# End of a MoE layer: order of mixing, turning, squaring and adding on three engines

## Chip, cores and metric
One core of one Trainium2 chip runs the whole program. The metric is device time in microseconds (us), here the median of the runs shown.

## What is computed
The reference chains two small diffusion-like blocks over 512 latent and 256 context tokens with D = 1024, all in float32. The second block has two layers; each ends with a hierarchical mixture of experts (top 2 of 32), whose result is gated and added to the residual stream. Cut to what matters:

```python
def hier_moe(h, ...):                      # h: tokens x 1024
    ...                                    # two experts and two weights per token
    yb = lax.map(expert_block, (buf.reshape(n_blk, BLK, d), blk_e))
    y = yb.reshape(n_rows, d)[dest] * sw[:, None].astype(h.dtype)
    return jnp.zeros_like(h).at[stok].add(y)
# end of layer 0: 256 context and 512 latent tokens; end of layer 1: 512 latent tokens
ctx = ctx + cgt2 * f[:, :c_len]
x = x + gt2 * f[:, c_len:]
```

Layer 1 begins with an RMS norm of both streams, so it needs the sum of squares of every token over its 1024 features. The output of the program is x after layer 1.

## The kernel before
The residual stream X lies in on-chip memory with features in the partitions: 8 feature tiles of 128, by 768 tokens. The experts write their rows to a scratch tensor `yb` in HBM, one row of 1024 per token and expert. The end of a MoE layer (class `Moe`) then goes by tiles of 128 tokens, 6 in layer 0 and 4 in layer 1. For a tile `tt`:

- GpSimd (queue POOL) gathers two tiles of rows, `GA[2*tt]` and `GA[2*tt+1]`, one indirect DMA each (L3203), the 12 or 8 of them one behind the other; each has a semaphore `got[i]`.
- ScalarE weighs the first: it multiplies its rows by the first expert's weight (L3030, semaphore `weighed`).
- VectorE mixes: second rows times second weight, plus the weighed first rows (L3063, semaphore `mixed`). Both operands lie in on-chip SBUF.
- TensorE turns the mixed tile in two groups of four 128x128 transposes into one PSUM bank each (L208, semaphore `mixturned`); there are 6 banks, so from the seventh group on it also waits for `added`.
- VectorE adds: for each of the 8 feature tiles, PSUM times gate plus X into X (L3069, semaphore `added`).

In layer 0 alone there is more (object `after`, class `TokenSums`): ScalarE squares the tile of X (L278, into one of two buffers, so the square of tile t waits for the sum of tile t-2), and TensorE sums the squares over features by 8 products with a matrix of ones (L202, 16 records in the trace). When all 6 sums are there, ScalarE takes the inverse root (L233, L235).

Each engine follows its own queue in the order written. ScalarE: all 6 weighings, then all 6 squares, then the root. VectorE: mixing 0, additions 0, mixing 1, additions 1, and so on. TensorE: turn 0, turn 1, sum 0, turn 2, sum 1, turn 3, ..., with sum t-2 ahead of turn t; the last two sums follow the last turn.

Beside that, SyncE loads the first two chunks (2 MB each) of the next layer's weights `w_in_c` as soon as the first bank is turned (L415, `all_used`); behind a barrier of all engines (L118) the third part of the program begins, which SyncE opens with the third chunk (L2334). In layer 1 SyncE stores the output of each tile when its additions are done (L3337, 512 KB each), and the program ends.

Of the kernel before, what the change touches and what calls it, by code (L numbers as in the profile page):

```python
# [9 lines left out]
ALU = mybir.AluOpType  # L10
ACT = mybir.ActivationFunctionType
# [194 lines left out]
def turn4(pe, bank, srcs, ident):  # L206
    for i, src in enumerate(srcs):
        ins = pe.transpose(bank[:, i * 128:(i + 1) * 128], src, ident)  # L208
    return ins
# [2392 lines left out]

def strips(pe, A, B, left, right0, right1, kt):

# [228 lines left out]
class Moe:  # L2833
# [124 lines left out]
    def pe(self, pe, after=None):  # L2958
        K, ps, H, tiles = self.K, self.K.ps, self.norm.H, self.tiles
        self.before.over(pe)  # L2960
        pe.wait_ge(self.tables, self.TABLES)
        for k in range(KT):
            self.norm.wait_tile(pe, k)
            for j, (a, n) in enumerate(self.segments()):
                ins = pe.matmul(ps[0:36, 2 + j, 0:n], self.wr[:, k, :], H[:, k, a:a + n], start=(k == 0), stop=(k == KT - 1), skip_group_check=True)  # L2965
                if k == KT - 1:
                    ins.then_inc(self.logits, 1)
        for tt in range(tiles):
            if tt in (0, 4):
                pe.wait_ge(self.levac[tt // 4], 1)  # L2970
            ins = pe.transpose(ps[:, 4, 36 * tt:36 * tt + 36], self.LT[0:36, 128 * tt:128 * tt + 128], K.C("ident")[0:36, 0:36])
        ins.then_inc(self.lturned, 1)
        self.pe_turn(pe, 0, 2)

        pe.wait_ge(self.masked, 2)
        n = 32 * (tiles + 1)
        flat = self.M.rearrange("p t e -> p (t e)")
        pe.matmul(ps[:, 2, 0:n], K.C("tri"), flat, start=True, stop=False, skip_group_check=True)
        for u in range(1, tiles + 1):
            ins = pe.matmul(ps[:, 2, 32 * u:n], K.C("ones"), flat[:, 0:n - 32 * u], start=False, stop=(u == tiles), skip_group_check=True)  # L2980
        ins.then_inc(self.counted, 1)
        self.pe_turn(pe, 2, tiles)
        for i in range(2 * tiles):
            pe.wait_ge(self.chosen, i + 1)
            ins = pe.matmul(ps[0:ROWS, 3, 0:self.NB], self.S[:, i, :], self.A[:, i, :], start=(i == 0), stop=(i == 2 * tiles - 1))
        ins.then_inc(self.listed, 1)
        pe.wait_ge(self.index, 1)
        pe.wait_ge(self.hevac, 2 * tiles)
        self.blocks.pe(pe)
        self.when_more(pe, self.more.pe)  # L2990
        for i in range(2 * tiles):
            tt, c = divmod(i, 2)
            pe.wait_ge(self.mixed, tt + 1)
            if i >= 6:
                pe.wait_ge(self.added, 4 * (i - 5))
            if after and c == 0 and tt >= 2:
                after.pe_sum(pe, tt - 2)
            turn4(pe, ps[:, 2 + i % 6, :], [self.GA[2 * tt][:, k * 128:(k + 1) * 128] for k in range(4 * c, 4 * c + 4)], K.C("ident")
                  ).then_inc(self.mixturned, 1)
        if after:  # L3000
            for tt in range(tiles - 2, tiles):
                after.pe_sum(pe, tt)
# [9 lines left out]
    def act(self, act, after=None):  # L3012
        K, ps = self.K, self.K.ps
        self.sums.act_root(act)
        self.norm.act_shift(act)
        act.wait_ge(self.logits, 1)
        act.activation(self.LT[0:36, 0:TX], ps[0:36, 2, :], ACT.Copy).then_inc(self.levac[0], 1)
        self.act_rows(act, 0, self.tiles)
        ex, ex8 = self.sm[:, :, 12:16], self.sm[:, :, 56:64]
        act.wait_ge(self.shifted, 1)  # L3020
        act.activation(ex, ex, ACT.Exp).then_inc(self.exped, 1)
        act.wait_ge(self.shifted, 2)
        act.activation(ex8, ex8, ACT.Exp).then_inc(self.exped, 1)
        self.blocks.act_engine(act)
        self.when_more(act, self.more.act_engine)
        act.wait_ge(self.experts, 3)
        for tt in range(self.tiles):
            A = self.GA[2 * tt]
            act.wait_ge(self.got[2 * tt], 16)
            act.activation(A, A, ACT.Copy, scale=self.WTS[:, 0, tt:tt + 1]).then_inc(self.weighed, 1)  # L3030
        if after:
            for tt in range(self.tiles):
                act.wait_ge(self.added, 8 * (tt + 1))
                after.act_square(act, tt)
            after.act_root(act)

    def dve(self, dve):
        K, ps, X, MOD = self.K, self.K.ps, self.K.X, self.norm.MOD
        self.before.over(dve)
        dve.memset(self.M[:, self.tiles, :], 0.0).then_inc(self.masked, 1)  # L3040
        self.norm.dve_gains(dve)
        self.norm.dve_scale(dve)
        if self.nt == T:
            dve.wait_ge(self.logits, 2)
            dve.tensor_copy(self.LT[0:36, TX:T], ps[0:36, 3, 0:TC]).then_inc(self.levac[1], 1)
        dve.wait_ge(self.lturned, 1)
        dve.tensor_tensor(self.L, ps[:, 4, 0:36 * self.tiles].rearrange("p (t n) -> p t n", n=36),
                          K.PR(f"rb{self.layer}").unsqueeze(1).broadcast_to([128, self.tiles, 36]), ALU.add).then_inc(self.logged, 1)
        dve.wait_ge(self.logged, 1)
        self.chain = Chain(self.gate)  # L3050
        self.dve_choice(dve)
        self.dve_places(dve)
        dve.wait_ge(self.listed, 1)
        dve.tensor_copy(self.IDX[0:ROWS, 0:self.NB], ps[0:ROWS, 3, 0:self.NB]).then_inc(self.index, 1)
        self.dve_more(dve)
        self.dve_weights(dve)
        self.blocks.dve(dve)
        self.when_more(dve, self.more.dve)
        for tt in range(self.tiles):
            A, B = self.GA[2 * tt:2 * tt + 2]  # L3060
            dve.wait_ge(self.got[2 * tt + 1], 16)
            dve.wait_ge(self.weighed, tt + 1)
            dve.scalar_tensor_tensor(A, B, self.WTS[:, 1, tt:tt + 1], A, ALU.mult, ALU.add).then_inc(self.mixed, 1)  # L3063
            for c in range(2):
                i = 2 * tt + c
                dve.wait_ge(self.mixturned, i + 1)
                for k in range(4):
                    m, at = 4 * c + k, slice(tt * 128, (tt + 1) * 128)
                    dve.scalar_tensor_tensor(X[:, m, at], ps[:, 2 + i % 6, k * 128:(k + 1) * 128], MOD[:, 40 + m, tt // 4:tt // 4 + 1], X[:, m, at],  # L3069
                                             ALU.mult, ALU.add).then_inc(self.added, 1)  # L3070

    def dve_choice(self, dve):

# [411 lines left out]
```

## Time and profile before

| | |
|---|---|
| time, median of 3 runs | 4271.62 us |
| lowest, highest | 4269.14, 4275.84 us |
| span of the profiled execution | 4284.5 us |
| PE busy | 3763.7 us (88% of the span) |
| DVE (VectorE) busy | 1536.8 us (36%) |
| ACT (ScalarE) busy | 1371.9 us (32%) |
| POOL (GpSimd) busy | 199.9 us (5%) |
| mean granted TensorE clock | 0.950 of full speed |

The profile gives no time of its own for the profiled execution beside its span, which runs from the first to the last instruction. Times in it are microseconds from the span's start. PE is TensorE's products and transposes, PEld its weight loads, SPq the queue of SyncE. "x8" are eight instructions merged into one line, with the time from the first one's start to the last one's end. In brackets stands how long the engine was idle before, and what released it; a releaser is inferred. The end of layer 0's MoE runs from some 3108 to 3169 us, that of layer 1 from some 4255 us to the end.

### The profile page before, as it was taken

What the parts mean: (1) busy time and instruction counts of PE and PEld (TensorE: products, weight loads), DVE (VectorE), ACT (ScalarE), POOL (GpSimd) and SP (SyncE); (2) the same over time, 40 slices, a digit from 0 to 9 for tenths busy, and PEclk for the clock granted to TensorE, in tenths of its full rate; (3) what the DMA queues carried; (4) which work ended last, traced back from release to release, by engine and by line L of the source; (5) the groups of instructions that cost most, each with busy time, mean ns of one, the idle gap of its engine ahead of it and who ended that gap; (6) DMA issues with size and microseconds to landing.
All of it is one profiled execution on the core that took longest, in us unless ns stands there. A gap on an engine that the chain in (4) does not pass through costs nothing. (4 is left out here: it accounts for less than half of the span.)

```text
span 4284.5 us, 75829 instructions
## 1 busy us (share of the span) xinstructions
PE 3763.7 (88%) x32214; PEld 2090.7 (49%) x32214; DVE 1536.8 (36%) x3723; ACT 1371.9 (32%) x2940; POOL 199.9 (5%) x193
## 2 busy tenths in 40 slices
PE   7998678787776998998988989999969988899997
PEld 4554566666665544564566543333345454333332
DVE  3011666666664103452257231111132183211112
ACT  2002244344433113442446222222235262222222
POOL 0000000000000001110200000000012000000000
PEclk9999799999998999999999989999979999899998
DMA  5223444444443110001110249999733102799996
GB/s 209 76 83 116 103 120 113 124 125 121 121 117 122 59 66 1 20 20 67 34 44 1 102 174 391 392 391 391 315 138 93 44 1 108 273 390 391 389 393 260
DMA packets 314586, 696.03 MB, mean 162 GB/s; under 512 B 169216, under 2 KB 195968, under 8 KB 289152
## 3 DMA queue, kind: packets, MB, share of 16 engines
q1 hardware_dynamic: 293024, 612.41, 40.1%
q0 software_dynamic: 14048, 53.49, 3.6%
q10 hardware_dynamic: 7168, 25.17, 1.5%
q8 instruction: 260, 4.26, 0.4%
q14 instruction: 86, 0.70, 0.1%
HBM read 624.94 MB, written 63.71 MB: 161 GB/s over the span
## 5 line engine op out<-in xcount | busy, mean ns | idle before, releaser
L202 PE MATMUL ps<-arena 128*128 128x512 f32 (+8 forms) x4620 | 1463.3, 481 | 81.9 <-ACT arena L1137 13.8
L202 PEld LDWEIGHTS ps<-arena 128*128 128x128 f32 (+5 forms) x4620 | 787.1, 190 | 693.9 <-issue 455.3
L2608 PE MATMUL ps<-arena 128*32 128x512 f32 x9216 | 1024.2, 597 | 33.1 <-DMA arena<-in_w 28.3
L2608 PEld LDWEIGHTS ps<-arena 128*32 128x32 f32 x9216 | 306.7, 110 | 652.8 <-issue 635.9
L620 PE MATMUL ps<-arena 64*64 64x64 f32 (+1 forms) x10624 | 459.4, 239 | 154.9 <-DVE arena L1290 40.3
L620 PEld LDWEIGHTS ps<-arena 64*64 64x64 f32 x10624 | 410.2, 144 | 241.1 <-issue 105.8
L2742 DVE COPY arena<-ps 128x384 f32<-128x384 f32 x64 | 35.7, 558 | 645.7 <-PE ps L2667 645.7
L208 PE MATMUL ps<-arena 128*128 128x128 f32 x1168 | 189.9, 297 | 84.3 <-DVE arena L3063 39.6
L2718 ACT ACTIVATE arena<-ps 96x512 f32<-96x512 f32 x64 | 38.0, 594 | 626.6 <-PE ps L2608 626.6
L208 PEld LDWEIGHTS ps<-arena 128*128 128x128 f32 x1168 | 141.1, 151 | 141.0 <-issue 44.7
L600 DVE SCALAR_TENSOR_TENSOR arena<-arena 128x769 f32<-128x769 f32 x48 | 45.7, 1016 | 277.0 <-PE ps L202 276.7
L962 PE MATMUL ps<-arena 64*64 64x64 f32 x2304 | 101.5, 245 | 37.6 <-DVE arena L1290 33.9
L400 DVE SCALAR_TENSOR_TENSOR arena<-ps,arena 128x512 f32<-128x512 f32 (+1 forms) x48 | 31.8, 662 | 286.3 <-PE ps L202 286.3
L2760 DVE TENSOR_TENSOR arena<-ps,arena 64x512 f32<-64x512 f32 x64 | 43.7, 683 | 226.5 <-ACT arena L2730 226.5
L552 ACT ACTIVATE arena<-ps 128x512 f32<-128x512 f32 x64 | 31.0, 491 | 281.2 <-PE ps L202 261.4
L2730 ACT ACTIVATE arena<-ps 64x512 f32<-64x512 f32 x64 | 38.0, 594 | 244.5 <-PE ps L2608 244.5
L962 PEld LDWEIGHTS ps<-arena 64*64 64x64 f32 x2304 | 89.2, 156 | 47.6 <-DVE arena L1290 39.5
L1748 DVE TENSOR_REDUCE arena<-ps 128x1 f32<-128x768 f32 x64 | 61.3, 958 | 142.3 <-PE ps L202 142.3
L344 PE MATMUL ps<-arena 128*128 128x512 f32 (+1 forms) x208 | 85.6, 576 | 20.8 <-ACT arena L335 20.8
L2773 POOL DMA_INDIRECT arena<-htok,arena x64 | 58.1, 908 | 932.5 <-PE ps L2667 922.0
L253 ACT ACTIVATE arena<-arena 128x768 f32<-128x768 f32 (+1 forms) x32 | 24.5, 785 | 233.7 <-DVE arena L400 233.7
L216 PE MATMUL ps<-arena 128*32 128x512 f32 x576 | 78.3, 667 | 19.9 <-DMA arena<-in_w_mod 16.9
(282 smaller groups left out, 3774.3 us busy)
## 6 DMA issues: line engine op xcount, KB each, us to landing
arena<-in_w SPq DMA_DIRECT2D x192, 2048.0 KB, 28.9
arena<-in_w_mod SPq DMA_DIRECT2D x24, 2048.0 KB
arena<-in_mod_w SPq DMA_DIRECT2D x12, 2048.0 KB
yb<-arena ACTq DMA_DIRECT2D x64, 384.0 KB, 9.9
arena<-in_rwkv_w_in SPq DMA_DIRECT2D x8, 2048.0 KB
arena<-rkvg SPq DMA_DIRECT2D x38, 384.0 KB, 4.2
rkvg<-arena POOLq DMA_DIRECT2D x32, 384.0 KB, 3.0
arena<-di SPq DMA_DIRECT2D x192, 64.0 KB, 2.6
```

Of the source, the lines that this page charges most:

```text
L202: ins = pe.matmul(out, l, r, start=(i == 0), stop=(i == len(pairs) - 1))
L208: ins = pe.transpose(bank[:, i * 128:(i + 1) * 128], src, ident)
L216: ins = pe.matmul(out[32 * j:32 * j + 32, :], cs[:, 4 * half + j, :], w[:, 4 * half + j, :], start=(half == 0), stop=(half == 1))
L344: ins = pe.matmul(out, w[:, k, :], self.H[:, k, a:a + n], start=(k == 0), stop=(k == KT - 1), skip_group_check=True)
L600: dve.scalar_tensor_tensor(self.LPs[j % 2][:, k, 1:n + 1], self.XX[:, k, 1:n + 1], self.K.PR("mu")[:, 8 * j + k:8 * j + k + 1], self.H[:, ...
L620: ins = pe.matmul(out[p, :], l[p, :], r[p, :], start=(i == 0), stop=(i == len(pairs) - 1))
L962: ins = pe.matmul(out[p, :], src[p, :], ident[p, p], start=True, stop=True)
L1748: dve.tensor_reduce(mx, self.scores(n), AX.XY, ALU.max).then_inc(self.max, 1)
L2608: return pe.matmul(bank[32 * at:32 * at + 32, :], left[:, k, 32 * g:32 * g + 32], right[:, k, :], start=first, stop=last)
L2718: act.activation(self.moe.AC[i % 2][0:ROWS, :], A[0:ROWS, :], ACT.Silu).then_inc(self.silu, 1)
L2760: dve.tensor_tensor(YS[0:64, 512:1024], ps[0:64, 7, :], YS[0:64, 512:1024], ALU.add).then_inc(self.y1, 1)
L2773: pool.indirect_dma_start(out=moe.HG[i % 3][0:ROWS, :], out_offset=None, in_=self.K.scr["htok"][0:moe.nt, :], in_offset=bass.IndirectOffse ...
```

## The change
Three orders change, in both layers; no instruction is added or removed.

- VectorE: mixing 0 stands ahead of the loop, and mixing tt+1 stands ahead of additions tt.
- ScalarE: three weighings first; then square tt (after additions tt), followed by weighing tt+3. Without `after` (layer 1) the weighings stand in a row as before.
- TensorE: sum tt-2 stands behind turn tt instead of ahead of it.

```diff
-        for i in range(2 * tiles):
-            tt, c = divmod(i, 2)
+        for tt in range(tiles):
             pe.wait_ge(self.mixed, tt + 1)
-            if i >= 6:
-                pe.wait_ge(self.added, 4 * (i - 5))
-            if after and c == 0 and tt >= 2:
+            for c in range(2):
+                i = 2 * tt + c
+                if i >= 6:
+                    pe.wait_ge(self.added, 4 * (i - 5))
+                turn4(pe, ps[:, 2 + i % 6, :], [self.GA[2 * tt][:, k * 128:(k + 1) * 128] for k in range(4 * c, 4 * c + 4)], K.C("ident")
+                      ).then_inc(self.mixturned, 1)
+            if after and tt >= 2:
                 after.pe_sum(pe, tt - 2)
-            turn4(pe, ps[:, 2 + i % 6, :], [self.GA[2 * tt][:, k * 128:(k + 1) * 128] for k in range(4 * c, 4 * c + 4)], K.C("ident")
-                  ).then_inc(self.mixturned, 1)
...
         act.wait_ge(self.experts, 3)
+        for tt in range(3):
+            self.act_weigh(act, tt)
         for tt in range(self.tiles):
-            A = self.GA[2 * tt]
-            act.wait_ge(self.got[2 * tt], 16)
-            act.activation(A, A, ACT.Copy, scale=self.WTS[:, 0, tt:tt + 1]).then_inc(self.weighed, 1)
-        if after:
-            for tt in range(self.tiles):
+            if after:
                 act.wait_ge(self.added, 8 * (tt + 1))
                 after.act_square(act, tt)
+            if tt + 3 < self.tiles:
+                self.act_weigh(act, tt + 3)
+        if after:
             after.act_root(act)
...
+        self.dve_mix(dve, 0)
         for tt in range(self.tiles):
-            A, B = self.GA[2 * tt:2 * tt + 2]
-            dve.wait_ge(self.got[2 * tt + 1], 16)
-            dve.wait_ge(self.weighed, tt + 1)
-            dve.scalar_tensor_tensor(A, B, self.WTS[:, 1, tt:tt + 1], A, ALU.mult, ALU.add).then_inc(self.mixed, 1)
+            if tt + 1 < self.tiles:
+                self.dve_mix(dve, tt + 1)
...
+    def dve_mix(self, dve, tt):
+        A, B = self.GA[2 * tt:2 * tt + 2]
+        dve.wait_ge(self.got[2 * tt + 1], 16)
+        dve.wait_ge(self.weighed, tt + 1)
+        dve.scalar_tensor_tensor(A, B, self.WTS[:, 1, tt:tt + 1], A, ALU.mult, ALU.add).then_inc(self.mixed, 1)
```

`act_weigh` holds the wait and the weighing of one tile, as `dve_mix` does for the mixing.

## Rows read from the trace of the kernel before

**Rows 1.** The page: the span of the profiled execution
```profile
span 4284.5 us, 75829 instructions
```

**Rows 2.** Timeline from 3110 us, layer 0: start, length, engine, line, operation [idle before <-releaser]
```profile
3116.18 1.28 DVE L3063 SCALAR_TENSOR_TENSOR arena<-arena 128x1024 f32<-128x1024 f32 x1 [13.40 <-DMA arena<-yb,arena]
...
3117.46 1.15 ACT L3030 ACTIVATE arena<-arena 128x1024 f32<-128x1024 f32 x1 [2.74 <-DMA arena<-yb,arena]
...
3117.53 1.97 PE L208 MATMUL ps<-arena 128*128 128x128 f32 x8 [16.12 <-DVE arena L3063]
3118.59 0.95 POOL L3203 DMA_INDIRECT arena<-yb,arena  x1 [0.30 <-issue]
...
3118.68 2.16 DVE L3069 SCALAR_TENSOR_TENSOR arena<-ps,arena 128x128 f32<-128x128 f32 x8 [1.21 <-PE ps L208]
...
3120.76 1.28 DVE L3063 SCALAR_TENSOR_TENSOR arena<-arena 128x1024 f32<-128x1024 f32 x1
3121.10 1.75 POOL L3203 DMA_INDIRECT arena<-yb,arena  x1 [0.30 <-issue]
...
3123.16 0.95 POOL L3203 DMA_INDIRECT arena<-yb,arena  x1 [0.30 <-issue]
...
3125.32 1.28 DVE L3063 SCALAR_TENSOR_TENSOR arena<-arena 128x1024 f32<-128x1024 f32 x1
3126.68 1.15 ACT L3030 ACTIVATE arena<-arena 128x1024 f32<-128x1024 f32 x1 [2.96 <-DMA arena<-yb,arena]
3130.76 1.15 ACT L3030 ACTIVATE arena<-arena 128x1024 f32<-128x1024 f32 x1 [2.93 <-DMA arena<-yb,arena]
3131.82 1.98 ACT L278 ACTIVATE arena<-arena 128x1024 f32<-128x1024 f32 x2
...
3133.00 3.75 PE L202 MATMUL ps<-arena 128*128 128x128 f32 x16 [8.94 <-ACT arena L278]
...
3136.54 1.91 PE L208 MATMUL ps<-arena 128*128 128x128 f32 x8
3137.64 2.16 DVE L3069 SCALAR_TENSOR_TENSOR arena<-ps,arena 128x128 f32<-128x128 f32 x8 [11.05 <-PE ps L208]
...
3157.74 1.86 PE L208 MATMUL ps<-arena 128*128 128x128 f32 x8
...
3159.43 1.95 PE L202 MATMUL ps<-arena 128*128 128x128 f32 x16
...
3162.14 2.05 PE L202 MATMUL ps<-arena 128*128 128x128 f32 x16 [0.76 <-ACT arena L278]
...
3169.07 0.37 SPq L2334 DMA_DIRECT2D arena<-in_w_in_c  x1
```

**Rows 3.** Who waited for whom, 3100 to 3170 us: total us, times, longest
```profile
ACT arena L278 <- DVE arena L3069: 24.1, 4, 6.2
DVE arena L3069 <- PE ps L208: 23.4, 5, 11.0
```

**Rows 4.** The gathers of L3203, 3100 to 3200 us: issue to landing
```profile
DMA to landing us min/median/max: 5.0/8.1/9.6
```

**Rows 5.** DMA share in tenths, 3118 to 3170 us, 40 slices of 1.3 us
```profile
DMA  9999999999999996000000000000000000000000
```

**Rows 6.** Busy us by stretch: length, PE, PEld, DVE, ACT, POOL, granted clock, DMA share, GB/s
```profile
3132.00:3138.00 6.00, 5.00 (x23) 5.03 (x24) 0.36 (x2) 1.80 (x2) 0.00 (x0) 0.50 1.04 383
...
3138.60:3139.40 0.80, 0.00 (x0) 0.00 (x0) 0.80 (x4) 0.00 (x0) 0.00 (x0) 0.80 0.13 44
```

**Rows 7.** Timeline of PE, 3655 to 3682 us: transposes of another stage
```profile
3656.23 1.97 PE L208 MATMUL ps<-arena 128*128 128x128 f32 x16
```

**Rows 8.** Timeline from 4250 us, layer 1
```profile
4263.82 1.15 ACT L3030 ACTIVATE arena<-arena 128x1024 f32<-128x1024 f32 x1 [3.68 <-DMA arena<-yb,arena]
...
4278.70 2.16 DVE L3069 SCALAR_TENSOR_TENSOR arena<-ps,arena 128x128 f32<-128x128 f32 x8 [1.21 <-PE ps L208]
```

**Rows 9.** DMA issued from 4278 us: the last store, size, issue to landing
```profile
out<-arena SPq DMA_DIRECT2D x1, 512.0 KB, 3.2
```

More of the change, by code:

```diff
@@ L3026, in act, with act_weigh @@
         act.wait_ge(self.experts, 3)
+        for tt in range(3):
+            self.act_weigh(act, tt)
         for tt in range(self.tiles):
-            A = self.GA[2 * tt]
-            act.wait_ge(self.got[2 * tt], 16)
-            act.activation(A, A, ACT.Copy, scale=self.WTS[:, 0, tt:tt + 1]).then_inc(self.weighed, 1)
-        if after:
-            for tt in range(self.tiles):
+            if after:
                 act.wait_ge(self.added, 8 * (tt + 1))
                 after.act_square(act, tt)
+            if tt + 3 < self.tiles:
+                self.act_weigh(act, tt + 3)
+        if after:
             after.act_root(act)
+    def act_weigh(self, act, tt):
+        A = self.GA[2 * tt]
+        act.wait_ge(self.got[2 * tt], 16)
+        act.activation(A, A, ACT.Copy, scale=self.WTS[:, 0, tt:tt + 1]).then_inc(self.weighed, 1)
     def dve(self, dve):
```

## The prediction

> **What bounds the kernel now.** I read three views in this order. First the timeline of the end of layer 0's MoE, from the first gather of expert outputs to the first instruction of the third part of the program [rows 2]; then who waited for whom in the same stretch [rows 3]; then the same timeline for layer 1, where the program ends [rows 8]. What the reader is to see: no engine is full here, and the engines wait on each other in a ring. For a token tile VectorE mixes two rows (L3063, 1.28 us), TensorE turns them (L208), VectorE adds them to X (L3069, 2.16 us for eight, the next instruction 2.07 us after the first of them). The mixing of the next tile is queued behind the additions, so TensorE begins to turn only when VectorE is through with both, and VectorE then waits 1.21 us for the first bank [rows 2]. That is 4.56 us a tile (3120.76 less 3116.18, less 0.02), for 3.35 us of VectorE's work.
>
> In layer 0 a second wait is worse. TensorE's program has "sum of squares of tile 0" ahead of "turn tile 2". ScalarE squares only after it has weighed all six tiles, the last at 3130.76, since its gather landed only then. So tile 2, mixed by 3126.60 (3125.32 + 1.28), is turned from 3136.54 on, and its additions begin at 3137.64, 11.0 us late [rows 2, 3]. After that, turning tile 3 waits for the sum of tile 1, and so on: ScalarE waits for additions 24.1 us in four pieces, VectorE for turned banks 23.4 us in five [rows 3]. The sixth tile's sum ends at 3164.19 (3162.14 + 2.05), the root follows, and the third part's first load is issued at 3169.07, 4.88 us behind the sum [rows 2]. All engines meet at a barrier there, and only the prefetch of w_in_c crosses it; so what layer 0's end gains, the program gains, unless that prefetch is late.
>
> **The change in layer 0, part by part.** Numbers count tiles from 0. Nothing is added or removed: 6 weighings, 6 squares, 6 mixings, 48 additions, 48 transposes and 6 sums stay; three orders change. I rebuild the timeline with the durations of rows 2. Where the rows are silent, a landing is taken between its neighbours.
>
> Head. Mixing 0 ends at 3117.46 as before, and the prefetch, released by the first turned bank, starts as before. Mixing 1 now stands before additions 0; it needs weighing 1 and the fourth gather, both there near 3118.7: weighing 1 ends at 3118.61, and it began when the third gather had landed, 3117.46; issues stand 1.26 us apart (two of them from 3118.59 to 3121.10), so I put the fourth landing 1.25 us behind the third [rows 2]. It runs 3118.7 to 3120.0, so additions 0 start 1.3 us later than now. Queued behind that new wait are the additions, square 0 and the weighing of tile 3. Mixing 2 at 3122.0, additions 1 at 3123.3, mixing 3 at 3125.4, additions 2 at 3126.7: 11 us earlier than now, since turn 2 (from 3123.35) no longer waits for a square.
>
> ScalarE. Square 0 goes at 3122.15 (1.05 us), weighing 3 then to 3124.4, ahead of mixing 3's need. Square 1 ends at 3126.55, weighing 4 at 3127.8 (its gather lands at 3126.65), square 2 at 3129.95, weighing 5 at 3131.9, its gather being late anyway [rows 2]. The squares put ahead of weighings cost nothing, because gathers cover them; without that cover each would cost 1.05 us.
>
> Tail. Gather eleven is the last of the twelve, issued at 3123.16 and landing 9.6 us later [rows 2, 4], at 3132.8. Mixing 5 can't start before, and it now stands ahead of additions 4. So the path from the last landing is: mixing 1.28, additions 4 and 5, 2.07 + 2.16, square 1.06, sum 1.95, in all 8.5 us, ending at 3141.3 with the small gaps. Against 3164.19 that is a gain of 22.9 us.
>
> Does TensorE keep up? It needs 1.95 us for a sum at full clock (from 3159.43) and 3.54 us from a sum's start to the turn's at the lower one (3136.54 less 3133.00) [rows 2]. A turn is 1.69 us to the next sum at the lower clock (3159.43 less 3157.74) and 0.98 us at the full one (1.97 for sixteen) [rows 2, 7]. In the trace the engine works without a pause from 3133.0 to 3138.4 at a granted clock of 0.50 (1.2 GHz), and the clock rises to 2.4 GHz between 3138.6 and 3139.4 [rows 6]. Now it would work without a pause from 3123.35: turn 2, then sum 0 at the lower clock, to 3128.85; a rise near 3129, if it comes as long after the start of the unbroken work as there. Then turn 3 to 3129.8, sum 1 to 3131.7, turn 4 to 3132.6, sum 2 to 3134.5, turn 5 to 3135.5, sum 3 to 3137.4, sum 4 to 3139.35, sum 5 to 3141.3. It keeps up, with additions 5's bank 0.6 us early.
>
> One cost the diff doesn't show. In the trace the mixing of 3120.76 overlaps the issue of a gather on POOL at 3121.10, and that issue takes 1.75 us where the others take 0.95: it ends 0.8 us after the mixing does [rows 2]. The new mixings 1 and 2 fall among the last four issues too, so the last gather is issued between 0 and 1.3 us later (nothing if only one issue is caught, as now; a mixing's length if two are). I take 0.5, nearer the row that has one caught. Layer 0: 22.9 less 0.5 is 22.4 us.
>
> The Trainium skill ("SBUF — State Buffer", section "Who interferes with whom") says that a VectorE instruction with two SBUF inputs and a GpSimd instruction that reads SBUF exclude each other for a whole instruction, and that the one issued first blocks the other. The trace agrees for one direction (the 1.75 us); by that rule mixing 1, coming 0.1 us after an issue at 3118.59, would itself be held up to 0.85 us, and so mixing 2. That speaks against mixing early; the sum by it would be 0.85 us worse for the first additions, most of which the 0.7 us that additions 4 wait for mixing 5 absorbs.
>
> **Layer 1** has four tiles, no squares and no sums, and its weighings come in the same order. Weighing 1 ends at 4264.97 (4263.82 + 1.15), and the fourth gather lands about then; so mixing 1 at 4265.1, additions 0 from 4266.4, mixing 2 at 4268.4, mixing 3 at 4271.8, additions 2 at 4273.1, additions 3 at 4275.1 where they now start at 4278.70 [rows 8]. A gain of 3.5 us: three waits of 1.21 us, less 0.1. Stores: the last one takes 3.2 us to land [rows 9]; the additions of tiles 2 and 3 now end 2.1 us apart instead of 4.6. If stores ran one behind the other that costs 1.1 us, if they overlap nothing; I take nothing, since the prefetch shows two issues of one queue with the sixteen engines full under both [rows 5], and keep 2.4 to 3.6.
>
> **Sum.** 22.4 + 3.5 = 25.9 us, against the profiled execution's span of 4284.5 us [rows 1]: 4258.6. That execution is 12.9 us longer than the median of the three timed runs, 4271.62, and nothing in the stretches above tells why; I take the difference off the median: 4245.7, say 4246. A difference under 0.2% (8.5 us) can't be told from none, the three runs alone being 6.7 us apart.
>
> **The rivals.**
> (a) TensorE stays at 1.2 GHz. For it: the clock is at 0.50 in the present stage until 3138.6 [rows 6], through two turns and a sum. Then TensorE is the bound from 3123.35: six sums at 3.54 and four turns at 1.69 are 28.0 us, ending near 3151.5, a gain of 12.7 in layer 0, 16.2 in all: 4255.5. Against it: its unbroken work would last 18 us or more, where the clock has risen behind 5.4 us of it [rows 6].
> (b) The gathers land later, since they share the DMA engines with the two prefetched chunks of 2 MB, which keep these full until some 3138.8 [rows 5]. At worst the last gather ends with them: 6 us later, 19.9 in all: 4251.7.
> (c) The gain is lost at the barrier: the third part would start at 3146.2, its weights having landed by 3138.8, so 7.4 us are to spare. To eat 18 us or more they would have to come 25 us later; 4265 to 4272.
> (d) Slower than before. The place is the wait that the change adds: additions of tile t stand behind mixing t+1 and so behind gather 2t+3. Everything after the last landing takes 8.5 us; the point from which the order loses in layer 0 is a landing at 3155.7, 23 us late, and 26 us late for the program, 35 to be measurable as slower. Price: one us per us beyond; 4282 with a landing 36 us late. Against: the DMA engines are idle from 3138.8.
> (e) That the change does nothing: it would need TensorE's turn 2 to wait still for a square; but the wait on it now stands behind both turned banks.
>
> **How the numbers follow.** Chances: forecast 0.64, (a) 0.17, (b) 0.12, (c) and (e) 0.05, (d) 0.02. The likeliest gives 4246, and 4244 to 4249 by its own terms (gain 26.5 down to 23). The range goes up past (b) and (a) to 4258 and down by the runs' scatter of some 3 us to 4241. Faster 0.93, same 0.05, slower 0.02.
>
> **What would show it.** In the changed trace: additions of tile 2 near 3127 instead of 3137.6; in steady state mixing and additions back to back on VectorE with no idle from PE L208; the wait of L278 for L3069 far under 24 us; the last mixing of layer 0 right at its gather's landing; the last sum's end near 3141; the granted clock at 1.0 from about 3129; in layer 1 additions 3.35 us apart. Wrong would be: a clock of 0.50 through to the last sum (a), POOL issues stretched two or three times, or an ACT table load between a square and a weighing (now there is none between L3030 and L278).

## The result, and the profile after

The changed kernel took 4241.35 us (median of five runs, 4239.21 to 4252.89), the kernel before, timed again beside it, 4269.29 us (five runs, 4265.18 to 4275.84). The ratio is 0.9933, with a 95% interval of 0.9914 to 0.9953: 20 to 37 us less. A second series of the changed kernel, on one chip with two experiments, gave 4250.41 us (4237.42 to 4255.8) against 4273.15 (4266.28 to 4285.7), ratio 0.9945 (0.9928 to 0.9963). So it is faster, by 0.6 to 0.7% and by about what was forecast (25.9 us); how much of the 28 us between the first two medians is the change's, the total can't tell. The stages can. The first view shows busy time by stretch, of the kernel before and then of the changed one; the columns are the stretch, its length, then busy us and instructions of PE, PEld, DVE, ACT and POOL, granted clock, DMA share and GB/s. The stretches are, in this order: the recurrence of the first part (L620); all up to the first gather of layer 0's end; layer 0's end, up to the third part's first load (L2334); the third part up to layer 1's first gather; layer 1's end.

```profile
423.30:1379.50 956.20, 736.82 (x13995) 593.67 (x13996) 620.02 (x1820) 370.89 (x1143) 0.00 (x0) 0.90 0.43 121
1379.50:3108.48 1728.98, 1600.86 (x10120) 804.33 (x10116) 504.44 (x1126) 567.68 (x1046) 95.95 (x82) 0.98 0.40 153
3108.48:3169.07 60.59, 26.60 (x144) 24.24 (x144) 20.20 (x54) 17.32 (x16) 12.27 (x12) 0.64 0.47 174
3169.07:4254.73 1085.66, 1005.61 (x6704) 438.93 (x6704) 302.74 (x579) 344.02 (x611) 65.34 (x53) 0.98 0.61 229
4254.73:4284.50 29.77, 7.88 (x32) 6.28 (x32) 13.50 (x36) 4.59 (x4) 7.77 (x8) 0.50 0.64 213
```

```profile
422.90:1361.30 938.40, 730.49 (x13995) 590.82 (x13996) 620.06 (x1820) 370.52 (x1143) 0.00 (x0) 0.91 0.44 123
1361.30:3090.71 1729.41, 1602.32 (x10120) 803.58 (x10114) 504.61 (x1126) 567.14 (x1046) 95.88 (x82) 0.97 0.41 153
3090.71:3129.91 39.20, 20.61 (x144) 19.11 (x144) 19.94 (x54) 17.33 (x16) 12.06 (x12) 0.76 0.73 269
3129.91:4212.63 1082.72, 1008.19 (x6704) 438.67 (x6704) 301.75 (x579) 343.76 (x611) 65.58 (x52) 0.97 0.61 230
4212.63:4238.80 26.17, 7.88 (x32) 6.27 (x32) 13.23 (x36) 4.60 (x4) 8.03 (x8) 0.50 0.73 243
```

Layer 0's end takes 39.2 us instead of 60.6, layer 1's 26.2 instead of 29.8. That is 21.4 + 3.6 = 25.0 us, and both lie in code that the change touches. The two spans differ by 45.7 us (4284.5 less 4238.8): another 17.8 us lie in the recurrence, which has the same instructions in both, and 2.9 in the third part. The change touches no code there, and the experiments show below how far these stages scatter.

Now the end of layer 0 in the changed kernel. Mixing is L3082 here, the additions L3075, the weighing L3042; L208 (turns), L202 (sums) and L278 (squares) keep their numbers. These lines answer to [rows 2]:

```profile
3100.75 1.28 DVE L3082 SCALAR_TENSOR_TENSOR arena<-arena 128x1024 f32<-128x1024 f32 x1 [1.25 <-DMA arena<-yb,arena]
...
3104.14 1.06 ACT L278 ACTIVATE arena<-arena 128x1024 f32<-128x1024 f32 x1 [0.83 <-DVE arena L3075]
...
3105.36 1.09 PE L208 MATMUL ps<-arena 128*128 128x128 f32 x8 [1.34 <-DVE arena L3082]
...
3106.28 1.95 PE L202 MATMUL ps<-arena 128*128 128x128 f32 x16
3107.29 1.28 DVE L3082 SCALAR_TENSOR_TENSOR arena<-arena 128x1024 f32<-128x1024 f32 x1
...
3108.48 2.15 DVE L3075 SCALAR_TENSOR_TENSOR arena<-ps,arena 128x128 f32<-128x128 f32 x8
...
3115.61 1.28 DVE L3082 SCALAR_TENSOR_TENSOR arena<-arena 128x1024 f32<-128x1024 f32 x1 [1.50 <-DMA arena<-yb,arena]
...
3116.95 1.50 PE L208 MATMUL ps<-arena 128*128 128x128 f32 x8 [1.98 <-DVE arena L3082]
...
3118.25 6.78 PE L202 MATMUL ps<-arena 128*128 128x128 f32 x48
...
3121.55 1.06 ACT L278 ACTIVATE arena<-arena 128x1024 f32<-128x1024 f32 x1 [1.50 <-PE ps L202]
...
3129.91 0.37 SPq L2334 DMA_DIRECT2D arena<-in_w_in_c  x1
```

What to see: from 3104 to 3112 mixing and additions stand back to back on VectorE, and a tile takes 3.27 us (3104.02 to 3107.29). Turn 2 (3105.36) begins 0.06 us after mixing 2 ends, and sum 0 follows it. Then the last mixing starts at 3115.61, 1.50 us after VectorE was free, for the landing of the last gather, and TensorE, idle for 1.98 us, starts turn 5 behind it. Who waited for whom, against [rows 3]: the squares' wait for additions has gone from 24.1 us to 6.1, and VectorE's wait for a turned bank, 23.4 us before, isn't in the answer any more.

```profile
DVE arena L3082 <- DMA arena<-yb,arena: 16.0, 3, 13.2
...
ACT arena L278 <- DVE arena L3075: 6.1, 4, 3.3
```

The gathers of layer 0 in the changed kernel from issue to landing, against [rows 4], and the granted clock (third figure from the right) behind the last mixing:

```profile
DMA to landing us min/median/max: 4.4/6.4/11.1
```

```profile
3117.00:3119.00 2.00, 2.00 (x12) 2.00 (x13) 2.00 (x9) 0.00 (x1) 0.00 (x0) 0.62 1.05 385
3119.00:3120.00 1.00, 1.00 (x7) 1.00 (x7) 1.00 (x5) 1.00 (x1) 0.00 (x0) 0.50 1.05 389
...
3123.00:3125.10 2.10, 2.03 (x19) 1.84 (x17) 0.00 (x0) 0.94 (x2) 0.00 (x0) 1.00 0.00 0
```

And layer 1, against [rows 8]: the last sixteen additions run as one piece, 4.22 us, without the 1.21 us in between.

```profile
4229.79 1.28 DVE L3082 SCALAR_TENSOR_TENSOR arena<-arena 128x1024 f32<-128x1024 f32 x1
4230.98 4.22 DVE L3075 SCALAR_TENSOR_TENSOR arena<-ps,arena 128x128 f32<-128x128 f32 x16
```

### The profile page after: what moved, and what is told of

Its sections match the earlier page's. It is cut to its first block and busy times, and to the rows that moved or that the text cites. A ratio compares the mean times of both kernels' runs of the same rounds, so it can differ in the third digit from the quotient of the medians.

```text
span 4238.8 us, 75824 instructions
## 1 busy us (share of the span) xinstructions
PE 3754.1 (89%) x32214; PEld 2081.2 (49%) x32214; DVE 1535.5 (36%) x3723; ACT 1370.6 (32%) x2940; POOL 200.0 (5%) x193
## 5 line engine op out<-in xcount | busy, mean ns | idle before, releaser
L202 PE MATMUL ps<-arena 128*128 128x512 f32 (+8 forms) x4620 | 1459.9, 480 | 65.3 <-ACT arena L1137 14.4
L202 PEld LDWEIGHTS ps<-arena 128*128 128x128 f32 (+5 forms) x4620 | 787.4, 191 | 673.9 <-issue 445.8
L2608 PE MATMUL ps<-arena 128*32 128x512 f32 x9216 | 1027.0, 599 | 27.3 <-DMA arena<-in_w 22.4
L620 PE MATMUL ps<-arena 64*64 64x64 f32 (+1 forms) x10624 | 458.7, 240 | 145.7 <-DVE arena L1290 40.4
L620 PEld LDWEIGHTS ps<-arena 64*64 64x64 f32 x10624 | 409.1, 144 | 229.5 <-issue 101.9
L208 PE MATMUL ps<-arena 128*128 128x128 f32 x1168 | 187.4, 295 | 81.9 <-DVE arena L3082 39.9
L208 PEld LDWEIGHTS ps<-arena 128*128 128x128 f32 x1168 | 138.4, 149 | 139.3 <-DVE arena L3082 44.3
L600 DVE SCALAR_TENSOR_TENSOR arena<-arena 128x769 f32<-128x769 f32 x48 | 45.7, 1017 | 276.6 <-PE ps L202 276.4
L400 DVE SCALAR_TENSOR_TENSOR arena<-ps,arena 128x512 f32<-128x512 f32 (+1 forms) x48 | 31.8, 662 | 286.4 <-PE ps L202 286.4
L962 PEld LDWEIGHTS ps<-arena 64*64 64x64 f32 x2304 | 86.5, 153 | 48.3 <-DVE arena L1290 39.9
L1717 ACT ACTIVATE arena<-ps 128x768 f32<-128x768 f32 x64 | 51.9, 810 | 127.1 <-PE ps L208 127.0
```

What stands on the lines that cost most here:

```text
L202: ins = pe.matmul(out, l, r, start=(i == 0), stop=(i == len(pairs) - 1))
L600: dve.scalar_tensor_tensor(self.LPs[j % 2][:, k, 1:n + 1], self.XX[:, k, 1:n + 1], self.K.PR("mu")[:, 8 * j + k:8 * j + k + 1], self.H[:, ...
L620: ins = pe.matmul(out[p, :], l[p, :], r[p, :], start=(i == 0), stop=(i == len(pairs) - 1))
L962: ins = pe.matmul(out[p, :], src[p, :], ident[p, p], start=True, stop=True)
L1717: act.activation(self.PT[j % 2].rearrange("p (b i) t -> p b (i t)", b=2), ps[:, 4:6, 0:384], ACT.Copy).then_inc(self.pt, 1)
L2608: return pe.matmul(bank[32 * at:32 * at + 32, :], left[:, k, 32 * g:32 * g + 32], right[:, k, :], start=first, stop=last)
```

## The experiments

All of them are judged by two lengths read from the trace, since they are steadier than the total: from the first gather's issue to the third part's first load (layer 0's end: 60.6 us before, 39.2 after), and from layer 1's first gather to the end (29.8 and 26.2).

**Two theories of why layer 0's end got shorter.** The one that the prediction puts first is a single wait at the head of TensorE's queue: turn 2 behind a sum whose square isn't there. The other takes the stage as a ring of three engines, in which each of the three old orders closes the ring in its own place. It came from reading the old code again after the result: there TensorE waits for mixing tt first and then runs sum tt-2, so a late mixing holds back a sum as well as a turn. Six kernels keep the six other mixtures of old and new orders. Each was profiled once; three executions of the changed order took 38.7, 39.2 and 39.9 us for layer 0's end, so differences of about 1 us between kernels say nothing.

*TensorE's order alone.* The parts of the change in `act` and `dve` are undone; of the diff there stays

```diff
             pe.wait_ge(self.mixed, tt + 1)
-            if after and c == 0 and tt >= 2:
-                after.pe_sum(pe, tt - 2)
             turn4(...)                          # both banks
+            if after and tt >= 2:
+                after.pe_sum(pe, tt - 2)
```

> TensorE's order alone is changed (turn tt ahead of sum tt-2); ScalarE and VectorE keep the order of before. Measured: the end of layer 0 from the first gather's issue to the third part's first load, 60.6 us before and 39.2 us after. Ring theory (each of the three orders closes the ring in its own place, and squares wait for the sixth weighing): squares can't start before the last weighing ends, some 23.4 us in, and mixing stands behind additions; 51 us, 48 to 53. Rival, the prediction's reading (the turn of tile 2 that waits for a square is what costs): most of the gain, 44 us or less. Layer 1, from the first gather's issue to the end: 29.8 us as before, in both.

Measured: 48.0 us, and 29.1 for layer 1. The timeline of this kernel (additions L3070):

```profile
3121.97 2.16 DVE L3070 SCALAR_TENSOR_TENSOR arena<-ps,arena 128x128 f32<-128x128 f32 x8 [1.21 <-PE ps L208]
...
3126.85 3.78 PE L202 MATMUL ps<-arena 128*128 128x128 f32 x16 [4.06 <-ACT arena L278]
...
3131.52 2.16 DVE L3070 SCALAR_TENSOR_TENSOR arena<-ps,arena 128x128 f32<-128x128 f32 x8 [6.20 <-PE ps L208]
```

Tile 2's additions (3121.97) no longer wait for a square, yet 12.6 us of 21.4 are won and not all: sum 0 starts behind the sixth weighing and the first square, at 3126.85; turn 3 now stands behind it, and the additions of tile 3 wait 6.20 us (3131.52).

*ScalarE's order alone.*

```diff
+        for tt in range(3):
+            self.act_weigh(act, tt)
         for tt in range(self.tiles):
-            (weigh tt, then all squares in a loop of their own)
+            (wait for additions tt, square tt)
+            if tt + 3 < self.tiles:
+                self.act_weigh(act, tt + 3)
```

> ScalarE's order alone is changed (squares between weighings). Ring theory: the 11 us wait of tile 2's additions goes, since square 0 is there by the time tile 2 is mixed, but each tile is still mixing, sum, turn, additions one behind the other, 7.0 us each from tile 2 on; 55 us, 51 to 57. Rival (the wait for the square is what costs): the wait is gone by this alone, 49 us or less. Layer 1 29.8 us in both.

Measured: 53.6 us, and 28.6 for layer 1. The prediction's "11.0 us late" is down to 4.20 us by this alone (3121.33), and still only 7.0 us are won. In this kernel mixing is L3069:

```profile
3121.33 2.16 DVE L3075 SCALAR_TENSOR_TENSOR arena<-ps,arena 128x128 f32<-128x128 f32 x8 [4.20 <-PE ps L208]
3123.41 1.28 DVE L3069 SCALAR_TENSOR_TENSOR arena<-arena 128x1024 f32<-128x1024 f32 x1
...
3124.74 3.79 PE L202 MATMUL ps<-arena 128*128 128x128 f32 x16 [3.01 <-DVE arena L3069]
...
3129.41 2.16 DVE L3075 SCALAR_TENSOR_TENSOR arena<-ps,arena 128x128 f32<-128x128 f32 x8 [4.73 <-PE ps L208]
```

There is the link of the ring that the prediction left out: mixing 3 at 3123.41, behind it sum 1 at 3124.74, released by the mixing, behind that turn 3, and additions 3 at 3129.41, for which VectorE waited 4.73 us. And TensorE, idle for 2.6 to 3.0 us in every round, runs this sum at the lower clock: 3.79 us, where one at full clock takes 1.95.

*VectorE's order alone.*

```diff
+        self.dve_mix(dve, 0)
         for tt in range(self.tiles):
-            (mix tt)
+            if tt + 1 < self.tiles:
+                self.dve_mix(dve, tt + 1)
             (additions tt)
```

> VectorE's order alone is changed (mixing one tile ahead). Ring theory: in the old TensorE order a sum stands behind the wait for the mixing of two tiles later, so mixing ahead takes the mixing out of each of the last tiles' rings, though squares start only after the sixth weighing: 52.5 us, 48 to 54. Rival: nothing of the 11 us wait goes and only 1.2 us a tile is saved, 56 us or more. Layer 1: all of its gain, 26.2 us, in both.

Measured: 48.4 us and 25.5. The 10.8 us wait of tile 2's additions stays whole (line L3068 here), and 12.2 us are won all the same, behind it: mixing 3 is done long before, so from sum 1 on sums and turns follow each other with pauses of at most 0.62 us, and at full clock.

```profile
3116.10 3.75 PE L202 MATMUL ps<-arena 128*128 128x128 f32 x16 [10.69 <-ACT arena L278]
...
3120.75 2.16 DVE L3068 SCALAR_TENSOR_TENSOR arena<-ps,arena 128x128 f32<-128x128 f32 x8 [10.83 <-PE ps L208]
...
3121.27 1.95 PE L202 MATMUL ps<-arena 128*128 128x128 f32 x16
...
3123.06 1.04 PE L208 MATMUL ps<-arena 128*128 128x128 f32 x8
```

This is what the first theory can't give: by it 56 us or more were expected here.

*ScalarE's and VectorE's orders, TensorE's as before.*

> ScalarE's and VectorE's orders are changed, TensorE's is that of before (sum tt-2 ahead of turn tt). Ring theory: square 0 is there when tile 2 is mixed, so the sum ahead of the turn costs its own 2 to 2.5 us once, and VectorE is a tile ahead: 39 to 43 us, so TensorE's order is worth 4 us at most. Rival (the head of TensorE's queue is what costs): 47 us or more. Layer 1: 26.2 us in both.

Measured: 40.0 us and 26.1. Sum 0 stands ahead of turn 2 and at the lower clock takes 3.78 us, which costs the additions of tile 2 (L3074) 1.46 us:

```profile
3110.10 3.78 PE L202 MATMUL ps<-arena 128*128 128x128 f32 x16 [1.29 <-DVE arena L3081]
...
3114.77 2.16 DVE L3074 SCALAR_TENSOR_TENSOR arena<-ps,arena 128x128 f32<-128x128 f32 x8 [1.46 <-PE ps L208]
```

So with the two others changed, TensorE's order is worth 0.8 us by the lengths, no more than the 38.7 to 39.9 us among which the changed order scatters, though alone it is worth 12.6. The head of TensorE's queue isn't what costs, once squares and mixings are early.

*TensorE's and ScalarE's orders*, and then *TensorE's and VectorE's*:

> TensorE's and ScalarE's orders are changed, VectorE's is that of before (mixing behind additions). Ring theory: mixing, first bank, additions follow each other, 4.56 us a tile for six tiles, then square and last sum: 43 us at full clock, up to 47 at the lower one; 39.2 if VectorE's order were worth nothing. Layer 1: 29.8 us, as before.

> TensorE's and VectorE's orders are changed, ScalarE squares after all six weighings as before. Ring theory: the additions of all tiles run as in the changed kernel, but the six squares start 23.4 us in, and sums 0 to 5 follow turns 2 to 5: 45 us at full clock, up to 50 at the lower one. If ScalarE's order were worth nothing, 39.2. Layer 1: 26.2 us.

Measured: 42.5 us (layer 1: 30.3), half a us below the expected range, and 45.7 us (layer 1: 26.1). In the first, mixings follow each other every 4.1 to 4.6 us from the first to the last, and the last one starts 29.9 us after the first gather's issue, 5.3 us behind the last landing: VectorE's order is the bound. In the second, five of six mixings have started 20.4 us after the first issue, and then additions (L3069 there) wait 7.55 us for a bank that is turned behind sum 0, whose square came after the sixth weighing:

```profile
3117.93 1.99 ACT L278 ACTIVATE arena<-arena 128x1024 f32<-128x1024 f32 x2
...
3119.02 3.78 PE L202 MATMUL ps<-arena 128*128 128x128 f32 x16 [8.25 <-ACT arena L278]
...
3123.70 2.16 DVE L3069 SCALAR_TENSOR_TENSOR arena<-ps,arena 128x128 f32<-128x128 f32 x8 [7.55 <-PE ps L208]
```

| orders changed | layer 0's end, us | gain |
|---|---|---|
| none | 60.6 | |
| TensorE | 48.0 | 12.6 |
| ScalarE | 53.6 | 7.0 |
| VectorE | 48.4 | 12.2 |
| TensorE, ScalarE | 42.5 | 18.1 |
| TensorE, VectorE | 45.7 | 14.9 |
| ScalarE, VectorE | 40.0 | 20.6 |
| all three | 39.2 | 21.4 |

The three single gains sum to 31.8 us, and together they give 21.4; the pair without TensorE gives nearly all. That is the ring theory, and the first theory falls: TensorE's order is worth 12.6 and 11.1 us (48.0 and 42.5 against 60.6 and 53.6) while mixings stand behind additions, 2.7 (45.7 against 48.4) where only squares are late, and 0.8 where neither is.

**What bounds the changed kernel.** One number differs from the change: the value at which the prefetch of `w_in_c` is released.

```diff
-        self.all_used = self.mixturned, 1
+        self.all_used = self.mixturned, 8
```

> The changed kernel, with the prefetch of the two chunks of w_in_c released by the eighth turned bank instead of the first. Theory (the last gathers land late because the prefetch shares the DMA engines with them, and the last mixing waits for that): the last gather lands 6.5 us after its issue instead of 11.1, mixing 5 waits for nothing, and the end of layer 0 takes 36.5 us, 36 to 37.5, instead of 39.2; the prefetch is done before the third part's first product asks for it. Rival (gathers land late because of their own queue of twelve issues): 39.2. Second rival (the prefetch then comes too late): longer than 39.2. Total against the kernel before: 25 us + 2.7 less, ratio 0.9935.

Measured: 36.8 us and 25.7; ratio to the kernel before 0.992 (0.9903 to 0.9937). Gathers in this kernel, issue to landing, and the last mixing with the last turn:

```profile
DMA to landing us min/median/max: 5.0/6.5/6.6
```

```profile
3130.82 1.28 DVE L3082 SCALAR_TENSOR_TENSOR arena<-arena 128x1024 f32<-128x1024 f32 x1
...
3132.16 1.09 PE L208 MATMUL ps<-arena 128*128 128x128 f32 x8 [0.18 <-DVE arena L3082]
```

The longest landing is 6.6 us instead of 11.1, the last mixing waits for nothing, and TensorE's pause ahead of turn 5 is 0.18 us instead of 1.98. The prefetch is done before the third part begins: the DMA engines are idle again from some 3140, the part's first load is issued at 3144.31. This is the shortest end of layer 0 of all that were run; by the total alone its 0.992 can't be told from the changed kernel's 0.9933 and 0.9945. So the bound that is left in the changed kernel is the one that the prediction named, the last landing, and its cause is the prefetch on the same DMA engines.

> The changed kernel, with sum 3 ahead of the wait for the last mixing instead of behind turn 5. Theory (in the changed kernel TensorE idles 1.98 us for the last mixing, then its granted clock falls to 0.50 from 3117.x to 3120.x and the last three sums and the turn take 8.1 us instead of 6.9): sum 3 fills most of that idle stretch, one sum less stands behind the last mixing, the clock stays at 1.0, and layer 0's end takes 38.3 us, 38.0 to 38.6, against 39.2. If the clock falls all the same, 38.8 or more. If the tail is bound by additions, square and sum alone, 39.2. Layer 1 26.2.

```diff
         for tt in range(tiles):
+            early = after and tt == tiles - 1
+            if early:
+                after.pe_sum(pe, tt - 2)
             pe.wait_ge(self.mixed, tt + 1)
...
-            if after and tt >= 2:
+            if after and tt >= 2 and not early:
```

Measured: 39.9 us and 25.6. As a whole that is a miss, by 1.5 us: the last gather landed 26.3 us after the first issue in this execution, 24.9 in that of the changed kernel. 1.1 of these 1.4 us are a later end of the last issue (16.5 against 15.4 us), since three issues were stretched there (1.22, 1.65 and 1.71 us), and one in the changed kernel's (1.63). Behind the last mixing:

```profile
3118.98 1.29 DVE L3085 SCALAR_TENSOR_TENSOR arena<-arena 128x1024 f32<-128x1024 f32 x1 [0.76 <-DMA arena<-yb,arena]
...
3121.25 1.04 PE L208 MATMUL ps<-arena 128*128 128x128 f32 x8
...
3123.48 4.12 PE L202 MATMUL ps<-arena 128*128 128x128 f32 x32 [1.20 <-ACT arena L278]
```

```profile
3123.50:3125.60 2.10, 2.08 (x17) 1.90 (x17) 0.90 (x4) 1.15 (x2) 0.00 (x0) 1.00 0.01 4
```

Sum 3 fills the pause, the granted clock stays at 1.00, and from the start of the last mixing to the end of the last sum it is 8.6 us (3118.98 to 3127.60), against 9.4 (3115.61 to 3125.03). But that isn't shown to be the new order's doing. In the changed kernel's second execution (`e11_after_again`, below), with sum 3 behind turn 5, TensorE idled 1.08 us ahead of turn 5, the granted clock stayed at 1.00 too, and the same path took 8.6 us (3112.11 to 3120.73):

```profile
3113.45 1.09 PE L208 MATMUL ps<-arena 128*128 128x128 f32 x8 [1.08 <-DVE arena L3082]
...
3116.61 4.12 PE L202 MATMUL ps<-arena 128*128 128x128 f32 x32 [0.28 <-ACT arena L278]
```

In the third (`e8_mix_psum`, the same in layer 0) it idled 2.39 us there, the clock fell to 0.50, and the path took 9.4. Sum 3 also delays turn 5: it starts 0.98 us after mixing 5's end (3121.25 less 3120.27), where it started 0.06 us after it. By these executions the new order saves at most the 0.8 us of a fallen clock, and nothing where the clock holds.

> The kernel with the late prefetch, and besides: the last tile's square and sum in two halves (each half behind four of the eight additions), and in layer 1 the last store in two halves, the first released by the first four additions. Ring theory (in the late-prefetch run TensorE runs turn 5, sums 3, 4 and 5 with 0.28 us of idle in between): the split square arrives 0.5 us earlier and finds TensorE at sum 4, so layer 0's end gains 0.1 to 0.3 us on 36.8. If additions, square and sum were the bound one behind the other, it gains 1.4 us, 35.4. Layer 1: the last half store holds 256 KB instead of 512, 25.0 to 25.7 us against 26.2 and 25.7 if the landing depends on its size, unchanged if it is all latency.

Cut to the two halves; the kernel also lets the last sum's fifth product wait for the second half, and releases the prefetch at the eighth bank.

```diff
+            for h in range(2):                       # last tile's square, half by half
+                act.wait_ge(self.added, 8 * t + 4 * (h + 1))
+                act.activation(self.SQ[t % 2][:, 4 * h:4 * h + 4, :], X[:, 4 * h:4 * h + 4, ...], ACT.Square).then_inc(self.sq, 1)
...
+            for h in range(2):                       # last tile's store in layer 1
+                sp.wait_ge(moe.added, 24 + 4 * (h + 1))
+                sp.dma_start(out[:, 4 * h:4 * h + 4, at], K.X[:, 4 * h:4 * h + 4, at]).then_inc(K.s["stored"], 16)
```

Measured: 36.8 us, as without the split, and 25.7 for layer 1; ratio 0.9931 (0.9913 to 0.995). The halves of the square (L281) ran one behind the other, since they share a buffer with sum 3 and waited for that:

```profile
3129.80 1.15 ACT L281 ACTIVATE arena<-arena 128x512 f32<-128x512 f32 x2 [0.64 <-PE ps L202]
```

So TensorE is the bound behind the last turn: turn 5 and three sums without a pause, 6.4 us from the turn's start (3126.94 to 3133.34), where the kernel without the split took 7.3 (3132.16 to 3139.43). That these 0.9 us don't show in the length has another reason: sum 0 ran at the lower clock for longer here (3.62 us instead of 2.54), and turn 5 started 25.5 us after the first gather's issue instead of 24.6. One execution of each can't tell what the split is worth. The smaller last store brought nothing beyond the scatter between executions (25.5 to 26.2 us in all that mix ahead).

**Is the rest scatter?** The changed kernel once more:

> The changed kernel itself, on one chip with the two others, for the scatter of what the change doesn't touch. Theory (executions differ in the first part's recurrence, which no part of the change touches: 956.2 us in the profiled run of before, 938.4 in that of the changed kernel, 942 to 952 in those of the experiments): the end of layer 0 takes 39.2 us and that of layer 1 26.2, both within 0.7, while the recurrence comes out anywhere from 938 to 956. Rival (the changed kernel's shorter time is in part an effect on other stages): the recurrence again near 938. Ratio to before 0.9941 by the stages alone (25.0 of 4271), 0.9933 by the first timing.

Measured: 38.7 us and 25.6, recurrence 942.5 us. Over all twelve profiled executions but that of the kernel before, the recurrence, which has the same instructions in each, took 938 to 952 us, and in no order that follows the edits: 948 with TensorE's order alone, 942 to 945 with two of the orders, 949 with both ends split. The kernel before had 956, in its one profile. The third part took 1082.7 to 1087.6 us, against 1085.7 before. So of the 17.8 us by which the first two profiles differ in the recurrence, 14 lie within what executions show that all have some part of the change; one profile of the kernel before can't settle the other 4. The 2.9 us of the third part lie within it whole. The long stretch between the recurrence and layer 0's end scatters too, from 1723 to 1733 us over all thirteen, with 1729 in both of the first two profiles. Layer 0's end in the changed order took 39.2, 38.7 and 39.9 us (the last in the next experiment); layer 1's took 25.5 to 26.2 us in nine executions that mix ahead and 28.6 to 30.3 in four that don't. The 25.0 us of the stages are a ratio of 0.9941 to 4271.62, inside both intervals.

**Does a mixing hold up a gather's issue, and by what?** In layer 1 alone:

```diff
+        if self.layer == 1:                      # A3, B3: A and B as 2 x 512
+            dve.scalar_tensor_tensor(A3, B3, self.WTS[:, 1, tt:tt + 1], self.K.ps[:, 0:2, :], ALU.mult, ALU.add)    # (cut)
```

> The changed kernel, but in layer 1 alone the mixing takes its second operand from a PSUM bank instead of the weighed rows in SBUF, so the first expert's rows are left out of layer 1's result. Disputed: the gather issue on POOL that overlaps a mixing takes 1.38 us in layer 1 of the changed kernel (issued 4221.41, mixing 4220.69 to 4221.97) where others take 0.94. If the second SBUF operand is the cause, that issue takes 0.94 us here, while the one in layer 0, where the mixing is as it was, still takes about 1.6. If VectorE's writes or its being busy are the cause, it stays at about 1.4. Layer 1 in all: within 0.5 us of 26.2 in either case, since that gather isn't waited for long.

Measured: 0.94 us for every issue that meets a mixing in layer 1 (26.2 us in all), and 1.71 us for the last issue of layer 0, where the mixing has both operands in SBUF. First layer 1 of the changed kernel, then of this one (mixing L3084):

```profile
4220.69 1.28 DVE L3082 SCALAR_TENSOR_TENSOR arena<-arena 128x1024 f32<-128x1024 f32 x1 [13.24 <-DMA arena<-yb,arena]
4221.41 1.38 POOL L3215 DMA_INDIRECT arena<-yb,arena  x1 [0.30 <-issue]
```

```profile
4235.78 1.28 DVE L3084 SCALAR_TENSOR_TENSOR arena<-arena,ps 128x1024 f32<-128x1024 f32 x1 [13.26 <-DMA arena<-yb,arena]
4236.50 0.94 POOL L3219 DMA_INDIRECT arena<-yb,arena  x1 [0.30 <-issue]
```

In both the issue comes 0.72 us into a mixing of 1.28 us. With two SBUF operands it ends 0.82 us after the mixing, with one it takes its 0.94 us. The second SBUF operand is the cause; it is one execution, but in all thirteen the 42 issues that start 0.19 to 1.13 us into a mixing with two SBUF operands end 0.81 to 0.83 us behind it.

## Why the prediction was right, and where it was wrong

**The mechanism and the two gains.** Layer 0 was put at 22.4 us and measured 21.4 (20.7 and 21.9 in two other executions); layer 1 at 3.5, measured 3.6. The sum of 25.9 stands against 25.0. Additions 2 start 17.8 us after the first gather's issue (3108.48 less 3090.71), where the rebuild had 18.2 (3126.7 less 3108.5). In layer 1 the stores overlap: the 1.1 us that they might have cost aren't there.

**The step that failed: the scatter.** The step is "down by the runs' scatter of some 3 us". The stages' measured gain puts the changed kernel at 4246.6 (4271.62 less 25.0); its median came 5.3 us below that in the first series and 3.8 us above it in the second (4250.41), which the stages that the change touches don't explain. The median of 4241.35 lies outside the 4244 to 4249 that the prediction gave by its own terms and 0.35 us above the low end of its whole range, which is luck: three of the eleven runs of the changed kernel in the two series lie below that end (4237.4, 4239.2 and 4240.5). The term was sized from three runs that lay 6.7 us apart. Single executions of one kernel lie up to 19 us apart (4266.3 to 4285.7 for before, 4237.4 to 4255.8 for the changed one), and 26 with the late prefetch (4234.2 to 4259.7). For the 12.9 us by which the profiled execution exceeded the median the prediction found no reason; its recurrence was the longest of all thirteen (956 us), but how long it was in the median execution no profile shows. Seen afterwards, 8 us on both sides of 4246 (4238 to 4254) hold both medians; the bounds were worked out for the mechanism and hardly at all for the yardstick.

**The reading of the old ring.** "After that, turning tile 3 waits for the sum of tile 1" is true and incomplete: the sum of tile 1 itself waited for mixing 3, by the order of two lines in the old code. The rebuild of the new order didn't need that link, so the number came out; an estimate of one part alone would not have. The prediction's stress on turn 2's 11 us wait would have put VectorE's order alone at 1.2 us a tile; it is worth 12.2 us in all.

**The last landing as the bound.** Right: the last mixing starts with it, and the 8.5 us path behind it is the path. It landed 24.9 us after the first issue, where the prediction had 24.3 and 0.5 more for a stretched issue. The sum is right by luck: the last issue ended no later than before (15.4 us after the first against 15.6), and the landing took longer, 11.1 us instead of 9.6. The 8.5 us were 9.4: "It keeps up" had TensorE's clock at full until the end. In fact it idled 1.98 us ahead of the last turn, the granted clock was 0.50 between 3119 and 3120, and the last three sums took 6.78 us instead of 5.85. By the rebuild's own numbers turn 5 could not start before 3134.1, and sum 2 was to fill the time until then, but with the clock up by turn 2 it was done 24.3 us after the first issue (3114.97) instead of 26.0, and the pause opened behind it. The two other executions of this order pause as well: 1.08 us, with the clock kept and 8.6 us behind the last mixing, and 2.39 us, with the clock down to 0.50 and 9.4.

**The rivals.** (a), TensorE at 1.2 GHz throughout, didn't come. The clock was at 1.00 from turn 2 to the pause (1.09 us for eight transposes at 3105.36, 14.7 us after the first issue; forecast for 20.5 us after it), and the engine had done two turns with pauses of 0.56 and 1.34 us before that. Behind the same two turns, turn 2 took 1.97 us in the two other executions of this order and with the late prefetch, and sum 0 took 3.29, 2.43 and 2.54 us instead of 1.95: there the clock rose during sum 0, 18 to 20 us after the first issue. The forecast was near those; what decides between them no run here tells. (b) came in part, 0.6 us instead of 6, and its cause is worth 2.4 us to remove. (c), (d) and (e) have no trace: the third part follows the last sum by the same 4.88 us, the latest landing in any kernel that mixes ahead is 26.3 us after the first issue, where (d) needed some 47, and turn 2 waits for nothing but mixing 2.

**The shared port.** The Trainium skill ("SBUF — State Buffer", "Who interferes with whom") was weighed with a mixing held up by an issue that came before it. That direction didn't show: at 3100.75 a mixing starts 0.01 us behind an issue at 3100.74 and takes its 1.28 us. Nor is that issue stretched (0.94 us). The other direction, the issue held by the mixing, showed in every run. By the same section of the Trainium skill a VectorE instruction with at most one SBUF input, outside the two-port modes, doesn't contend; the experiment with one SBUF operand agrees (0.94 us).

## What to carry to other kernels

Where engines wait for each other in a ring, write down for each instruction everything that stands ahead of it in its own queue, waits included, and price a reordering on the rebuilt ring, not by the longest single wait: here the longest wait (11.0 us) could stay whole while 12.2 us were won behind it. When the ring is gone, the next bound is what lands last; a prefetch released a little later (here by seven banks) was worth some 2 to 3 us, where TensorE's order as the third of the three was worth 0.8. And size the range by what the same kernel does from run to run in stages that the change never touches, before the change's own bounds.

## What the runs showed of the hardware that was not expected

- A gather issued from POOL takes 0.94 us. If it starts 0.19 to 1.13 us into a VectorE mixing of 1.28 us with two SBUF operands, it ends 0.81 to 0.83 us after the mixing, so it takes 0.98 to 1.91 us (42 issues in thirteen executions). The three that start only 0.01 to 0.08 us into one take 0.94, and so does the one that meets a mixing with one operand from PSUM.
- Twelve gathers beside two loads of 2 MB land up to 11.1 us after their issue, without them 6.5 us; the loads were issued later than eight of the gathers and still slowed the last five (7.1 to 11.1 us).
- A sum of squares takes 1.95 us at a granted clock of 1.00 and 3.8 at 0.50. With pauses of 2.6 to 3.0 us in each round (ScalarE's order alone) sums 0 to 3 took 3.67, 3.79, 2.49 and 2.46 us; with pauses of at most 0.62 us behind sum 0 (VectorE's order alone) 3.75 for sum 0 and 1.95 to 2.05 for the rest. The order alone doesn't fix it: in three executions of the changed order sum 0 took 1.95, 2.43 and 3.29 us, and the clock fell behind pauses of 1.98 and 2.39 us and not behind one of 1.08.
- The recurrence, 13,995 products and as many weight loads in small pieces, took 938 to 956 us in thirteen executions; why, no run here tells.
